# Four of the gate tiles moved out of an attention's steps into two more pairs of seven block products

## The reference, cut to what matters

```python
h = rms_norm(x, norm_g)
u = h @ w_in        # v_c, b_c, c_c, z_c (1024 each), q (1024), k, v (256 each), z_a (1024), gates (2 x 1024)
y_c = b_c * conv3(c_c * v_c) * silu(z_c);  y_a = y_c @ w_conv_out
o = sliding_window_attention(rms(q), rms(k), v, sinks) * silu(z_a);  y_b = o @ w_attn_out
g_a, g_b = split(sigmoid(gate_logits + gate_b))
x = x + (g_a * y_a + g_b * y_b) @ w_out
```

## Time and profile before

| | |
|---|---|
| median of 3 runs | 2362.17 us (2362.13 to 2363.04) |
| the profiled execution | 2360.81 us |
| its span, first to last instruction | 2359.1 us |
| granted TensorE clock, mean | 0.998 |
| busy: TensorE, VectorE, ScalarE, GpSimd | 2336.9, 1577.2, 1008.4, 147.0 us |
| DMA | 226.39 MB, 96 GB/s mean |

### The profile page before, as it was taken

One profiled execution on the slowest core, in us unless ns is written; L12 is line 12 of the kernel. 1 busy time (PEld: TensorE's weight loads), 2 busy tenths in 40 slices (PEclk: granted clock), 3 DMA queues, 4 the chain that ended last, 5 costly groups with the idle time before them and its releaser, 6 DMA issues.

```text
span 2359.1 us, 30617 instructions
## 1 busy us (share of the span) xinstructions
PE 2336.9 (99%) x11228; PEld 1945.3 (82%) x11228; DVE 1577.2 (67%) x2485; ACT 1008.4 (43%) x1743; POOL 147.0 (6%) x203
## 2 busy tenths in 40 slices
PE   8999999999999999999999999999999999999998
PEld 6778888888888888887788888998888888888886
DVE  6759998567777767636555753473698888883345
ACT  6347666343443434422233353463455444452124
POOL 1000000100000021121000030011100000000000
PEclk9999999999999999999999999999999999999999
DMA  5112232452322264511110042371122222243323
GB/s 199 45 45 72 81 119 70 143 125 85 103 90 86 84 232 126 166 48 52 43 49 23 27 153 81 92 239 54 54 72 80 80 80 87 91 153 121 101 63 125
DMA packets 254610, 226.39 MB, mean 96 GB/s; under 512 B 7470, under 2 KB 225795, under 8 KB 253474
## 3 DMA queue, kind: packets, MB, share of 16 engines
q1 hardware_dynamic: 233920, 148.39, 20.8%
q0 software_dynamic: 16672, 60.73, 8.0%
q10 hardware_dynamic: 3906, 15.78, 2.0%
HBM read 174.54 MB, written 50.33 MB: 95 GB/s over the span
## 4 chain that ended last, share of the span: by engine, by line
PE 93%; DVE 4%; ACT 1%; issue 1%; DMA 1%; SPq 0%; ACTq 0%; DVEq 0%
PE bank L1106 9%; PE bank L1108 9%; PE bank L1107 9%; PE bank L1764 5%; PE bank L1763 5%; PE bank L1765 4%; PE bank L1339 4%; PE bank L1340 4%; PE bank L1341 4%; PE bank L1290 3%; PE bank L1291 3%; PE bank L1289 3%; PE bank L1805 2%; PE bank L1806 2%; PE bank L1804 2%; PE bank L1574 1%
## 5 line engine op out<-in xcount | busy, mean ns | idle before, releaser
L1879 ACT ACTIVATE whi<-wraw 128x1024 fp32r<-128x1024 f32 (+2 forms) x147 | 147.9, 1006 | 404.0 <-PE bank L1108 186.3
L2913 DVE TENSOR_TENSOR wlo<-wraw,whi 128x1024 fp32r<-128x1024 f32 (+1 forms) x162 | 189.9, 1172 | 118.3 <-ACT whi L1879 112.3
L1289 PE MATMUL bank<-xhi,whi 128*128 128x512 f32 x320 | 124.7, 390 | 0.0
L1291 PE MATMUL bank<-xhi,wlo 128*128 128x512 f32 x320 | 124.6, 389 | 0.0
L1290 PE MATMUL bank<-xlo,whi 128*128 128x512 f32 x320 | 124.6, 389 | 0.0
L1106 PE MATMUL bank<-x2hi,whi 128*128 128x512 f32 x240 | 93.9, 391 | 0.0
L1107 PE MATMUL bank<-x2lo,whi 128*128 128x512 f32 x240 | 93.4, 389 | 0.0
L1108 PE MATMUL bank<-x2hi,wlo 128*128 128x512 f32 x240 | 93.4, 389 | 0.0
L1804 PE MATMUL bank<-ffn_hi,whi 128*128 128x512 f32 x240 | 93.4, 389 | 0.0
L1805 PE MATMUL bank<-ffn_lo,whi 128*128 128x512 f32 x240 | 93.4, 389 | 0.0
L1806 PE MATMUL bank<-ffn_hi,wlo 128*128 128x512 f32 x240 | 93.4, 389 | 0.0
(11 more groups left out here) (588 smaller groups left out, 6793.6 us busy)
## 6 DMA issues: line engine op xcount, KB each, us to landing
wraw<-in_w_in_dram SPq DMA_DIRECT2D x85, 512.0 KB, 3.9
wraw<-in_ffn_w_up_dram SPq DMA_DIRECT2D x44, 512.0 KB, 3.8
ffn_spill<-ffn_value SPq DMA_DIRECT2D x22, 512.0 KB, 3.5
filler_spill<-filler POOLq DMA_DIRECT2D x20, 512.0 KB, 3.0
wraw<-in_xattn_wkv_dram SPq DMA_DIRECT2D x16, 512.0 KB, 4.0
wraw<-in_ffn_w_down_dram SPq DMA_DIRECT2D x16, 512.0 KB, 4.1
ffn_raw<-ffn_spill ACTq DMA_DIRECT2D x14, 512.0 KB, 4.5
wraw<-in_ffn_w_down_dram SPq DMA_DIRECT2D x16, 384.0 KB, 3.5
```

The lines of the kernel that those rows point to most:

```text
L1289: pe.matmul(ps(fill_bank(m)), whi[slot][:, k, :], xh, start=(k == 0), stop=False)
L1291: last = pe.matmul(ps(fill_bank(m)), wlo[slot][:, k, :], xh, start=False, stop=(k == KT - 1))
L1879: act.activation(whi[slot][:, 0:n, 0:m], wraw[slot][:, 0:n, 0:m], ACT.Copy).then_inc(s_whi, 1)
L2913: dve.tensor_tensor(wlo[slot][:, 0:n, :], wraw[slot][:, 0:n, :], whi[slot][:, 0:n, :].bitcast(F32), ALU.subtract).then_inc(s_wlo, 1)
```

## The change

Gate tiles 4 and 5 of either gate leave the list of fillers and form two pairs with each other, ahead of the pairs of tiles 6 and 7. 12 filler tiles stand among attention's steps (6 steps, 18 matmuls a unit), 4 in its tail; the seven-product pairs are 18 instead of 16, of which four are gate tiles. The last line follows the semaphores' counts: with four extra pairs, all four of the fillers' semaphores get one more store. Nothing that is computed changes but the order of the sums in the four moved tiles.

```diff
-FILL_TILES = [Z_A + n for n in range(8)] + [G_B + n for n in range(6)] + [G_A + n for n in range(6)]
-EXTRA_PAIRS = ((G_B + 6, G_B + 7), (G_A + 6, G_A + 7))
+FILL_TILES = [Z_A + n for n in range(8)] + [G_B + n for n in range(4)] + [G_A + n for n in range(4)]
+EXTRA_PAIRS = tuple((g + n, g + n + 1) for n in (4, 6) for g in (G_B, G_A))
 FILLERS = len(FILL_TILES)
-FILL_IN = 16
+FILL_IN = 12
 FILL_STEPS = 2 * KT
 UNITS = 4 * NB
...
         RING = 16 * FILLERS // 4
-        BACK = (RING + 16, RING + 16, RING, RING, 16 * 3, 16 * KT, 16 * KT, 32 * KT)
+        BACK = (RING + 16, RING + 16, RING + 16, RING + 16, 16 * 3, 16 * KT, 16 * KT, 32 * KT)
```

## The result

| | before | after |
|---|---|---|
| median of 4 runs | 2362.15 us | 2382.31 us (2381.2 to 2384.11) |
| profiled execution | 2360.81 | 2381.21 |
| its span | 2359.1 | 2379.5 |

The account below looks back on a forecast made before the run. TensorE was taken as the bound, VectorE setting attention's beat after the change. Attention 23.1 us shorter, pairs 38.0 longer: net +14.9 on 2360.81 gives 2375.7 profiled; with 1.4 for the median, 2377.1 us, range 2368 to 2386.

Parts of the forecast that it names:

- TensorE's work: Whole kernel: four tiles leave attention, 43.6 us, two pairs return, 38.0 us; store hand-overs cost 0, 1 us at most.
- The beat: Attention: VectorE sets each unit's time, 7.30 us of work plus 0.22 waiting, taken as 7.5, against TensorE's 6.82.
- The first two units: Start of attention: no such dependence on VectorE, so they keep TensorE's full 1.36 us each, 2.7 us.
- The sum: Attention 23.1 us shorter (20.4 from thirty units, 2.7 from the first two), pairs give back 38.0: net +14.9 us.
- What would show it: Signs listed beforehand in attention's beat, engine waits, pairs and landmarks that would mark the forecast right or wrong.
- the pairs at 19 us: Convolution's pairs: their products were to keep 19.0 us each.
- the exponentials' waits in two of four units: Attention: VectorE waits for the small exponential where no evacuation precedes the scaling, 0.31 and 0.55 us.
- TensorE's waits for the sum of o: Attention: part of some 20 us of TensorE idle time was to be ended by the sum of o.
- The first one: Attention: VectorE sets the beat but loses no time to the exponentials; 7.27 us, net +8.0, 2370.2 us; chance 0.15.
- The second one: Attention: TensorE stays the bound, VectorE's unit below 6.82 us; net -5.6, 2356.6 us; chance 0.04.
- The third one: Attention: loop of scaling, transposes, weighted sum, rounding, low half sets the beat; 7.9 us, net +26.9, 2389 us; chance 0.12.
- The clock: Attention: TensorE's granted clock falls for lack of work; at half the clock net over +100 us; chance 0.01.

Follow-up runs that it names:

- the last kernel above: Changed kernel with 14 filler tiles among the steps, evacuations and splits ahead of two forms, VectorE's copy left out, one scaling on ScalarE: 2363.09 us, ratio 1.0004.

## Why the prediction was right, and where it was off

*TensorE's work.* Right. 43.6 us out and 38.0 in (38.1 by the landmarks); no copy and no product waited for the stores, for which 0 was taken.

*The beat.* The mechanism was right: VectorE sets it, 0.77 us above the 6.82 that TensorE needs. The term was mis-sized a little. Forecast were 7.30 us of work and 0.22 of waiting, rounded down to 7.5; it came to 7.59, of which the two waits listed for VectorE are 0.27 (3.4 and 0.3 us in 14 units), so 7.32 of its own. Over the 29 units behind unit 1 this is 2.7 us.

*The first two units.* Wrong: the step was that they have no dependence on VectorE and keep TensorE's full 1.36 us each. With the next unit's 0.68 us that puts the transposes of unit 1 3.4 us earlier; they came 1.5 us earlier (185.69 to 184.16 us), 1.9 us less. TensorE waited for VectorE there already: 0.58 us before the transposes of unit 0 for the inverse roots of q, 0.97 before those of unit 1 for the scaling, and twice 0.26 for the low half of q. The kernel before had no such waits.

*The sum.* Attention got 18.5 us shorter, not 23.1: the two terms above, 2.7 and 1.9 us. That is 4.6 of the 5.3 us by which the forecast missed; 0.8 lies far behind the change.

*What would show it.* The beat of 7.4 to 7.7, the pairs at 19 us, the exponentials' waits in two of four units all came. TensorE's waits for the sum of o, of which it spoke, did not: the list has the scaling (13.6 us) and the low half of q (1.5 us). The convolution's first product was to come 23 us earlier and came 18.5. The window's 60.79 of 65 us is 94% for VectorE, where over 95% was said. TensorE's listed waits are 15.7 us in attention, less than the 25.1 that it lost (43.6 - 18.5). A matmul's record lasts 0.39 us where the next one starts after 0.227, so the first 0.16 us of each stop count as busy: some 5 us for the 30 listed stops. Most of the rest is in matmuls that start a little later without a listed wait: from the first transposes to those of unit 30 the eight transposes of a unit take 24.6 us in all where they took 22.9, and the scores 0.9 us more.

*The rivals.* The first one, no time lost to the exponentials, is out by the 0.24 us a unit that VectorE waited for them. The second one, TensorE as the bound, was ruled out by the unit of 7.1 us of mere busy time, and rightly. The third one, the loop, I put at 7.9 us; it is there, but lower: with 8 tiles the beat followed VectorE's work down to 7.4, and it is where VectorE's operations stand between low half and scaling that it is felt, so that 0.2 us of relief gave 0.09 and moving work there gave next to nothing. A number for the loop alone no run gives. The clock stayed at 1.00 in attention.

The Trainium skill ("Perfetto Trace Analysis", Identifying the Most-Contended Engine) judges TensorE's headroom by the weight loads' busy share and not by the matmuls', and calls the engine with the highest share the most contended. In attention before that is VectorE, 91% against 86%. The measurement differs for that kernel: 0.33 us more of VectorE's work in each unit cost it nothing, so TensorE set its pace. The rule did name the engine that set it once filler had left. The weight loads' share alone does not tell whether TensorE waits: it was 86% before and 87% in the last kernel above (91.08 of 105 us), where TensorE never waited, and 77% in the changed one (50.23 of 65 us), where it did.

## What to carry to other kernels

Ask of each block of work that is moved what it covered while it stood there, and work out the beat of the stage for every engine, waits included, before counting the saving. Where a filler is taken away, the second engine's own time per step is the floor, and the loop of waits through all engines is the next one; relief of the one alone brought half of what it took off here. A tail that looks like spare work may be hiding a reload: count what must land before it ends.

## What the runs showed of the hardware

TensorE's granted clock is less steady than the times suggest. During 9.8 us of waiting it fell to 0.50. With 8 tiles among the steps, where TensorE was busy for 49 of 60 us, it fell for some 3.4 us four times in attention, though no wait there was longer than 1.6 us (one of 1.9 lies 30 us earlier); with 12 tiles (60.4 of 65 us) it stayed at 1.00. And in 7 of the 13 profiled executions, but not in those of the kernel before and the changed one, it fell for 3.4 or 6.8 us in the second layer, from between 1165 and 1217 us, in a place that no edit touched: within 0.7 us of the start of the last of eight small matmuls that contract over 64 or 32 partitions. All 13 have these matmuls, so they alone don't decide it; what does is open. Timeline of TensorE, run with 14 tiles:

```profile
1169.64 0.39 PE L1108 MATMUL bank<-x2hi,wlo 128*128 128x512 f32 x1
1169.96 0.50 PE L1477 MATMUL bank<-gate_low_parts,gk_w_hi 64*128 64x512 f32 x1
...
1173.19 0.79 PE L1478 MATMUL bank<-gate_low_parts,gk_w_lo 32*128 32x512 f32 x1
...
1174.93 0.63 PE L1108 MATMUL bank<-x2hi,wlo 128*128 128x512 f32 x1
```

Here the level is 0.50 from 1172.6 to 1179.4 us, and the next 512-wide matmuls start about 0.43 us apart. At half speed a fall costs up to half its length, 1.7 or 3.4 us, which is as large as several effects of this study; so the beats, not the times alone, carry the argument above. Whether the two slower of the changed kernel's four runs (2383.4 and 2384.11 against 2381.2) had such a fall is open: their mean clocks over the whole run, 0.997 and 0.998 against 0.998 and 0.999, would allow one and don't show it.
